# The attention's steps go between halves of the input projection's units, and the scan of layer 0 takes two modulation units a head

## What is computed

```python
sh1, sc1, g1, sh2, sc2, g2 = split(silu(c) @ w_mod + b_mod)     # the modulation, per layer
h = modulate(rms_norm(x), sh1, sc1);  hc = the same of the context
ua, us, um = split_in(h @ w_in)       # attention, short convolution, scan
# attention (4 heads): q from rms_norm(ua[:256]) @ w_uq, k and v from rms_norm(ua[256:384]) @ w_ukv,
#   32 further columns, rotated, are the same for all heads' keys
y_att = softmax(q k^T * scale) v       # over 512 keys (context and x)
# short convolution: gate_b, gate_c, val = split(us)
y_sc = gate_b * dwconv(gate_c * val)
# scan (8 heads of 64, 2 groups, chunks of 128): z, xbc, dt = split(um)
xs, B, C = split(silu(dwconv(xbc) + bias));  la = -softplus(dt + bias) * exp(a_log)
cs = cumsum(la) in a chunk
y = (C B^T * exp(cs_i - cs_j)) (xs * dt) + C state * exp(cs), in both directions
y_ssd = norm((y + d * xs) * silu(z))
x = x + g1 * rms_norm(concat(y_att, y_sc, y_ssd) @ w_out)
x = x + g2 * rms_norm(square(relu(h2 @ w_ff1)) @ w_ff2)
```

## Time and profile before

| what | value |
|---|---|
| time, median of 3 runs | 1649.65 us (1649.46 to 1651.49) |
| the profiled execution | 1653.87 us, its span 1652.1 us |
| mean granted clock of TensorE | 0.962 |
| busy: PE, DVE, ACT, POOL | 93%, 60%, 55%, 4% of the span |
| layer 0: input projection's units from bc on | 69.4 to 161.6 us |
| layer 0: attention, and the scan to its last pair | to 216.3, and to 274 us |
| layer 1: attention | 820.3 to 855.5 us |

### The profile page before, as it was taken

How to read it: one execution, slowest core, us unless ns; L and a number is a source line. 1 busy time by engine, 2 the same in 40 slices (tenths; PEclk the granted TensorE clock), 3 DMA queues, 4 the chain that set the end, 5 groups by cost and what they waited for, 6 DMA issues and landing times.

```text
span 1652.1 us, 25531 instructions
## 1 busy us (share of the span) xinstructions
PE 1530.2 (93%) x10131; PEld 1281.4 (78%) x10131; DVE 985.0 (60%) x1579; ACT 911.5 (55%) x1506; POOL 71.6 (4%) x106
## 2 busy tenths in 40 slices
PE   5999988979999999979988899998999999888887
PEld 3687445748888888838855799998999999888787
DVE  2463568484343434474767766667776767577555
ACT  5653656463241323454565655556786868377745
POOL 3000023000000000000002000000000000001200
PEclk9999889989999999999987999999999999999899
DMA  7731435332523232342316566553644434343332
GB/s 248 231 102 51 153 128 180 127 128 77 178 80 99 101 103 99 110 131 83 123 31 200 179 210 198 194 190 128 217 147 154 154 128 154 103 153 105 100 102 77
DMA packets 223639, 225.38 MB, mean 136 GB/s; under 512 B 8234, under 2 KB 222064, under 8 KB 223472
## 3 DMA queue, kind: packets, MB, share of 16 engines
q1 hardware_dynamic: 222816, 223.63, 41.9%
q0 software_dynamic: 704, 0.12, 0.0%
HBM read 222.68 MB, written 1.05 MB: 135 GB/s over the span
## 4 chain that ended last, share of the span: by engine, by line
PE 75%; DVE 12%; ACT 10%; issue 2%; DMA 1%; SPq 0%; POOL 0%; DVEq 0%; ACTq 0%; POOLq 0%
PE bank L1046 21%; PE bank L1048 21%; PE bank L1047 21%; PE bank L1094 2%; ACT SH L1724 2%; ACT whi L1588 1%; DVE wlo L2151 1%; PE bank L1252 1%; PE bank L1412 1%; DVE AP L2715 1%; PE bank L1440 1%; PE bank L1367 1%; ACT AP L2005 1%; DMA raw<-in_w_out_dram 1%; PE bank L1345 1%
## 5 line engine op out<-in xcount | busy, mean ns | idle before, releaser
L2151 DVE TENSOR_TENSOR wlo<-raw,whi 128x1024 fp32r<-128x1024 f32 (+2 forms) x322 | 388.2, 1209 | 260.0 <-ACT whi L1588 255.2
L1588 ACT ACTIVATE whi<-raw 128x1024 fp32r<-128x1024 f32 (+2 forms) x322 | 336.0, 1046 | 273.2 <-PE bank L1048 251.4
L1046 PE MATMUL bank<-HH,whi 128*128 128x512 f32 (+2 forms) x640 | 245.8, 384 | 18.3 <-DVE HL L2173 15.2
L1047 PE MATMUL bank<-HL,whi 128*128 128x512 f32 (+2 forms) x640 | 241.7, 378 | 0.0
L1048 PE MATMUL bank<-HH,wlo 128*128 128x512 f32 (+2 forms) x640 | 241.4, 377 | 0.0
L1046 PE MATMUL bank<-HA,whi 128*128 128x256 f32 x576 | 166.1, 288 | 13.5 <-DVE LA L2173 5.2
L1047 PE MATMUL bank<-LA,whi 128*128 128x256 f32 x576 | 163.0, 283 | 0.0
L1048 PE MATMUL bank<-HA,wlo 128*128 128x256 f32 x576 | 162.9, 283 | 0.0
L1046 PEld LDWEIGHTS bank<-HH,whi 128*128 128x128 f32 (+1 forms) x640 | 120.8, 189 | 47.9 <-issue 16.6
L1048 PEld LDWEIGHTS bank<-HH,wlo 128*128 128x128 f32 (+1 forms) x640 | 120.9, 189 | 23.5 <-issue 0.5
L1047 PEld LDWEIGHTS bank<-HL,whi 128*128 128x128 f32 (+1 forms) x640 | 121.2, 189 | 22.6 <-issue 0.9
(11 more groups left out here) (375 smaller groups left out, 3141.8 us busy)
## 6 DMA issues: line engine op xcount, KB each, us to landing
raw<-in_w_ff_dram SPq DMA_DIRECT2D x64, 1024.0 KB, 5.4
raw<-in_w_mod_dram SPq DMA_DIRECT2D x48, 1024.0 KB, 5.3
raw<-in_a_w_in_dram SPq DMA_DIRECT2D x40, 1024.0 KB, 5.1
raw<-in_w_in_dram SPq DMA_DIRECT2D x18, 1024.0 KB, 5.4
raw<-in_b_w_in_dram SPq DMA_DIRECT2D x9, 1024.0 KB, 5.3
raw<-in_w_out_dram SPq DMA_DIRECT2D x8, 1024.0 KB, 5.3
raw<-in_ple_w_gate_dram SPq DMA_DIRECT2D x8, 1024.0 KB, 5.2
raw<-in_a_w_out_dram SPq DMA_DIRECT2D x4, 1024.0 KB, 5.1
```

The source lines that it names most:

```text
L1046: nc.tensor.matmul(o, wh, xh, start=start, stop=False, skip_group_check=shared)
L1047: nc.tensor.matmul(o, wh, xl, start=False, stop=False, skip_group_check=shared)
L1588: f(whi[h % HALF_SLOTS][:, 0:n], raw[u.id % RAW_SLOTS][:, (h % 2) * n:(h % 2) * n + n], ACT.Copy)\
L2151: v.tensor_tensor(wlo[h % HALF_SLOTS][:, 0:n], raw[u.id % RAW_SLOTS][:, (h % 2) * n:(h % 2) * n + n], whi[h % HALF_SLOTS][:, 0:n].bitcast( ...
```

## The change

- `mla_square` stands behind bc and `mla_norm` behind xs0, each a unit earlier.
- `mla_proj` is split into `mla_q` and `mla_k`, between the halves of xs1, and `mla_v`, between the halves of gc, with `ssd_cs` part 0. Two heads' keys share a bank, in two halves of 64 partitions.
- `ssd_dt` stands behind xs1, `ssd_cs` part 1 behind gc.
- The steps of `mla_att` stand between and behind the halves of val, gb, z0 and, in layer 0, z1; then `ssd_tok`.
- The seven fillers of layer 0's attention are gone; after the states and after each head 1 to 7 of its scan stand two. 17 stand in this scan instead of 9, and one fewer in its second feed-forward product.
- In layer 1, C is projected, convolved and multiplied for x alone.
- gate_b is no more copied by ACT: DVE multiplies by the bank, behind the convolution, and z0's silu waits for this.
- QT, KT, VV, PR and PT, TP and GC have other places in memory; POOL fills TP's pads in a memset of its own.

Its core as a diff:

```diff
 FILL = {
-    "mla": ((1, (1, 8)), (0, (1, 24))),
+    "win": ((0, (1, 8)), (0, (1, 24))),
+    "odd": ((0, (1, 8)), (0, (1, 24))),
     "g": ((1, (1, 8)), (1, (1, 20))),
-    "head": ((1, (1, 8)), (1, (1, 20))),
+    "head": ((2, (1, 8)), (1, (1, 20))),
...
-        fm(w, 0, COL_XBC + 512, 256, two, "win", (l, "bc"), x, [ALL] * 2)
-        fm(w, 0, COL_XBC, 256, two, "win", (l, "xs0"), x, [ALL] * 2)
+        win(COL_XBC + 512, "bc", [ALL, t1])
         steps.append(("mla_square", l))
-        fm(w, 0, COL_XBC + 256, 256, two, "win", (l, "xs1"), x, [ALL] * 2)
+        win(COL_XBC, "xs0", [ALL] * 2)
         steps.append(("mla_norm", l))
-        fm(w, 0, COL_GC, 256, two, "win", (l, "gc"), x, [t1] * 2)
-        fm(w, 0, COL_VAL, 256, two, "win", (l, "val"), x, [t1] * 2)
+        win(COL_XBC + 256, "xs1", [ALL] * 2, ("mla_q", l), ("mla_k", l))
         if l == 0:
             steps.append(("consts",))
         steps.append(("ssd_dt", l))
-        fm(w, 0, COL_GB, 256, two, "win", (l, "gb"), x, [t1] * 2)
-        fm(w, 0, COL_Z, 256, two, "win", (l, "z0"), x, [t1] * 2)
-        steps.append(("ssd_cs", l))
+        win(COL_GC, "gc", [t1] * 2, ("mla_v", l), ("ssd_cs", l, 0))
+        steps.append(("ssd_cs", l, 1))
+        steps.append(step(0))
+        win(COL_VAL, "val", [t1] * 2, step(1))
+        filler(*FILL["win"][l])
+        steps.append(step(2))
         steps.append(("short_conv", l))
-        fm(w, 0, COL_Z + 256, 256, two, "win", (l, "z1"), x, [t1] * 2)
+        win(COL_GB, "gb", [t1] * 2, step(3))
...
+        if l == 0:
+            win(COL_Z + 256, "z1", [t1] * 2, step(7), step(8))
...
-            for h in range(MLA_HEADS):
-                b = acquire(3 + h, (s_kt, (l, h)))
-                nc.tensor.matmul(b[0:NOPE, 0:T], w_ukv[:, h * P:h * P + NOPE], CK, start=True, stop=True)\
-                    .then_inc(*s_mla_k.tick((l, h)))
+            for p in range(MLA_HEADS // 2):
+                b = acquire(3 + p, (s_kt, (l, 2 * p + 1)))
+                for e in (0, 1):
+                    h = 2 * p + e
+                    ins = nc.tensor.matmul(b[NOPE * e:NOPE * e + NOPE, 0:T], w_ukv[:, h * P:h * P + NOPE], CK, start=True, stop=True)
+                ins.then_inc(*s_mla_k.tick((l, 2 * p), (l, 2 * p + 1)))
...
+        def mla_v(l):
+
+            run_late()
+            for j in range(4):
+                act.wait_ge(s_mla_v, s_mla_v.at((l, j)))
+                f(VV[:, j, :], banks[(7, 3, 4, 5)[j]][:, 0:256], ACT.Copy).then_inc(*s_vv.tick((l, j)))
...
+                elif part == "gb":
+                    for bi in (0, 1):
+                        y = YM[:, 2 + bi, :]
+                        v.tensor_tensor(y, y, bank(u, bi), ALU.mult).then_inc(*s_sc.tick((l, bi)))
```

More of the change, by code:

```diff
@@ L528, in lone_mod, with filler @@
         return u
+    fill = [(0, i) for i in range(8, 24)] + [(1, i) for i in range(0, 24)]
+    def filler(n, upto):
+        for _ in range(n):
+            if fill and fill[0] < upto:
+                ll, i = fill.pop(0)
+                mod_units(ll, i, i + 1)
     def w_in_units(l, opening):
@@ L534, in w_in_units, with at_half, win, step @@
             steps.append(("unit", u))
[L535 to L536 removed]
+        att = [(l, 2 * p + e, sg) for p in range(MLA_HEADS // 2) for sg in ((0, 1) if l == 0 else (1,)) for e in (0, 1)]
+        def at_half(part, *here):
+            if part != "z1":
+                steps.append(("split_to", 2 * next_sid() + 1))
+            for step in here:
+                steps.append(step)
+        def win(col, part, t, *here):
+            fm(w, 0, col, 256, two, "win", (l, part), x, t, (lambda: at_half(part, *here)) if here else None)
+        def step(i):
+            return ("mla_att", att, i)
+        win(COL_XBC + 512, "bc", [ALL, t1])
         steps.append(("mla_square", l))
[L538 removed]
+        win(COL_XBC, "xs0", [ALL] * 2)
         steps.append(("mla_norm", l))
[L540 to L541 removed]
+        win(COL_XBC + 256, "xs1", [ALL] * 2, ("mla_q", l), ("mla_k", l))
         if l == 0:
@@ L683, in build @@
             filler(*FILL["head"][l])
+            if h % 2 == 1:
+                filler(*FILL["odd"][l])
         def out_unit(i):
@@ L1534, in _ @@
                 mla_norm(*args)
-            elif kind == "mla_proj":
-                mla_proj(*args)
+            elif kind == "mla_q":
+                mla_q(*args)
+            elif kind == "mla_k":
+                mla_k(*args)
+            elif kind == "mla_v":
+                mla_v(*args)
             elif kind == "mla_att":
@@ L1904, in ssd_dt, with ssd_cs @@
             f(AA[:, 0, :], a_log[:, l, :], ACT.Exp).then_inc(*s_aa.tick(l))
-        def ssd_cs(l):
+        def ssd_cs(l, part):
+            if part == 0:
+                return
             act.wait_ge(s_df, s_df.at(l))
@@ L2245, in unit @@
                             .then_inc(*s_val.tick((l, "val", bi)))
+                elif part == "gb" and u.packed:
+                    y = YM[:, 2:4, SEQ:T]
+                    v.tensor_tensor(y, y, both(bank(u, 1)), ALU.mult).then_inc(*s_sc.tick((l, 0), (l, 1)))
+                elif part == "gb":
+                    for bi in (0, 1):
+                        y = YM[:, 2 + bi, :]
+                        v.tensor_tensor(y, y, bank(u, bi), ALU.mult).then_inc(*s_sc.tick((l, bi)))
                 elif part in ("bc", "xs0", "xs1"):
@@ L2899, in _ @@
                     nc.gpsimd.memset(XP0, 0.0)
-                    nc.gpsimd.memset(XP1, 0.0)
-                    nc.gpsimd.memset(TP, 0.0).then_inc(*s_pads.tick(l))
+                    nc.gpsimd.memset(XP1, 0.0).then_inc(*s_pads.tick(l))
+            elif kind == "unit" and args[0].kind == "win" and args[0].key[1] == "xs0":
+                l = args[0].key[0]
+                pool.wait_ge(s_parts, s_parts.at((l, "mix", KC - 1)))
+                nc.gpsimd.memset(TPW, 0.0).then_inc(*s_tp_pads.tick(l))
             elif kind == "att2_second" and args[0][0] == 1:
```

144 lines of the change are left out of this document (78 added, 66 removed).

## The result

The changed kernel takes 1670.83 us in the median of 4 runs (1668.46 to 1677.42), against 1649.84 (1649.46 to 1651.49) for the kernel before. The ratio is 1.0126, with a 95% interval of 1.0099 to 1.0153: slower by 21 us. The forecast was 1668, with a chance of 0.76 for slower. The profiled execution of the changed kernel is its fastest run, 1668.46 us, so the two traces differ by only 14.6 us of span. The four runs of the kernel before lie unusually close together: in the 11 to 23 runs that stand beside the experiments its median is 1650.6 to 1654.7 us, and against those the change costs 16 to 20 us and not 21.

What follows compares the result with a forecast made beforehand. PE's queue was taken to bound the kernel: layer 0 attention 0, its scan +13, ff2 -1.3, layer 1 +6.5, together +18.2, so 1672.1 us on the profiled execution and, 4.2 lower, 1667.9 as median. Range for 8 in 10: 1652 to 1680.

Steps and rivals of the forecast that it cites:

- The wait before `mla_q`: Attention, both layers: PE waits for DVE's queries (QC), 3.6 us in layer 0 and about 2.8 in layer 1.
- The wait before `ssd_cs`: Middle of gc, both layers: PE waits for LA and ACT's VV copies, 8 us in layer 0, about 9 in layer 1.
- the rival on the other side: Faster: PE's work covers the wait before `ssd_cs` in both layers, 25 us less, time 1643; chance of faster 0.17.
- The decision point: The change turns to a gain when the `ssd_cs` stops of both layers together cost less than 7 us.
- The clock behind these waits: Attention, both layers: a slow stretch behind each of the four new waits, 4 us each, 16 in all.
- `mla_k` and the halves of layer 1: Smaller PE work: `mla_k` saves 1.7 us in each layer; in layer 1 bc saves 2.7 and the g matmuls 0.9.
- The scan of layer 0: Eight more modulation units on PE, two in a slot: +13 us, bounds +2 and +18.
- the reason that I gave for the even heads: Layer 0's scan: the pick waits for ACT's mod_row copy, 3.84 us behind the rows; even heads 6.5 instead of 3.17.
- bound by something slower: Rival, layer 0's scan: 4 MB of transfers or DVE's modT banks make a pair of heads 14.5 us: +5, 1673; chance 0.12.
- my own case: The forecast's own case, 1661 to 1674 us, chance 0.52; in layer 0's scan, heads of 6.5 us each.
- The scan of layer 1: Half-width g matmuls give back 0.9 us; modulation order as before, DVE's halved copies under PE.
- The drain at each change of set: ACT's table loads: a skill's rule adds about 1.38 us per change, time near 1676; the sum left it out.

Runs made afterwards that it cites:

- e7: The changed kernel with xs1 whole and ssd_dt (bank 7 instead of 5), mla_q and mla_k behind it: 1654.42 us, ratio 0.9998 to the kernel before.
- e4: The changed kernel with mla_v and both parts of ssd_cs between the halves of val instead of gc, attention's step 0 ahead of them: 1664.08 us.
- e6: The changed kernel with ssd_cs part 0 moved from between the halves of gc to behind gc, mla_v left in place: 1662.90 us.
- e8: e7 with ssd_cs part 0 behind gc and attention's step 0 between its two parts: 1639.88 us, ratio 0.9936 to the kernel before.
- e1: The kernel before, its order kept, with only the change's smaller arithmetic (shared key banks, layer 1's C for x alone): 1648.66 us, ratio 0.9973.
- e2: The changed kernel, but ACT copies a head's modulation rows ahead of the next head's exponentials instead of behind them: 1669.51 us.
- e10: e9 with four of layer 0's modulation units moved from its scan's even heads to behind val, gb, z0 and z1: 1632.72 us, ratio 0.9879.
- e12: e10 with DVE's recurrence back ahead of head 1's modulation units: 1635.79 us, ratio 0.9900 to the kernel before.
- e3: The changed kernel with one modulation unit a head in layer 0's scan, and eight between the units of layer 0's input projection: 1670.82 us.
- e9: e8 with DVE's recurrence (ssd_rec) behind head 1's modulation units instead of ahead of them: 1644.09 us, ratio 0.9925 to the kernel before.
- e11: e1 with DVE's recurrence behind the unit of head 1, as in e9: 1652.25 us, ratio 0.9983.
- e5: The changed kernel with two modulation units ahead of xs1 in each layer, and fewer in the scans (13 instead of 17 in layer 0): 1667.42 us.

## Why the prediction was right, and where it was off

- *The wait before `mla_q`*: 3.6 and 2.8 forecast, 3.17 and 2.69 measured. e7 takes it away.
- *The wait before `ssd_cs`*: 8 and 9 forecast, 6.50 and 5.98 measured, ended by ACT's VV as forecast, and 0.69 and 3.13 for XR just ahead of it. Together these are 7.2 and 9.1, so the sum was met; that the last matmul of the values waits for XR stands in the order shown above the forecast, and the forecast did not price it apart. e7 shows the cause: with the dt chain and the convolution of xs1 beside q's matmuls instead of behind its copies, `ssd_cs` comes 10 us earlier. More cover alone helps less: of the 16.3 us some 14 are left in e4, in other places, and 11 in e6. So the rival on the other side named the right place: two stops and the clock behind them. The decision point held as well: with them smaller (2.0 and 4.4 us), e7 is level with the kernel before, and e8 is faster.
- *The clock behind these waits*: mis-sized. I took 4 us for each of four. Measured were 1.4 and 2.9 in layer 0, and 1.4 and 3.6 in layer 1: 9.3 for 16. A slow stretch often covers part of the wait itself, where nothing is lost: the first of layer 0 begins at 102.1 us, 0.6 before its wait ends, and the second of layer 1 lasts from 812.1 to 825.8, with the wait of 5.98 inside. These 6.7 us are most of the 3.5 and 3.8 us by which the two attention stretches came out better than forecast.
- *`mla_k` and the halves of layer 1*: 7.4 us of work by e1, 7.0 forecast (1.7 + 1.7 + 2.7 + 0.9).
- *The scan of layer 0*: +13.7 for +13. From the scan's first row to head 3 it is 7.1 us longer (30.1 for 23.0), where 3.9 were forecast, and from head 3 to head 7 6.5 longer (25.7 for 19.2), where 9.2 were (2 x 3.3 + 2 x 1.3). Some 3 us of this are one slow stretch behind the wait for the recurrence, which both kernels have and which now falls ahead of head 3 and not behind it; without it the two parts are +4.0 and +9.3. The last slot is 0.1 longer for a forecast of -0.1, but by luck: the wait of 4.04 is gone altogether, where I took 1.4 off, and 3.4 us of clock, for which the sum has no term, come in its place. Nor is the reason that I gave for the even heads the only one. The picks behind ACT's copies do wait, as e2's edit shows, only a transfer stands right behind them: the rival "bound by something slower" and my own case were both true at once, at 6.3 and 6.5 us a head. The units do not cost alike: by e10 and e12 the four in the even heads cost 9.6 and 9.8 us, and a scan with 13 units (56.8, 58.8) is only some 2 to 5 slower than one with 9 (54.0, 55.1 in e3).
- *The scan of layer 1*: -0.9 forecast, +3.9 measured. This was not foreseen. The clock is at its lower level for 21 us at a stretch, where before there were two with full clock between:

```profile
884.00:894.00 10.00, 9.37 (x58) 5.05 (x58) 5.39 (x15) 2.19 (x7) 2.18 (x3) 0.50 0.48 156
894.00:905.00 11.00, 11.00 (x63) 5.94 (x63) 2.41 (x7) 5.10 (x14) 2.90 (x4) 0.53 0.60 192
```

  The same stretch of before:

```profile
873.00:880.00 7.00, 7.00 (x47) 3.82 (x39) 4.55 (x12) 2.02 (x6) 2.17 (x3) 0.52 0.48 154
880.00:890.00 10.00, 8.08 (x73) 4.80 (x69) 3.10 (x8) 5.40 (x15) 2.92 (x4) 1.00 0.88 280
890.00:901.00 11.00, 9.74 (x58) 6.17 (x59) 10.25 (x20) 9.58 (x23) 5.01 (x5) 0.53 0.68 220
```

  The instructions of this stretch are the same but for the narrower products of C and B, and the wait ahead of it is 2.3 us (2.9 before). Over the scan PE loses 10.9 us to the clock (7.5 before) and is idle for 8.4 (6.7 before). The loss of time shows only at the end: the last pair but one starts 39.8 us behind the first row (39.7 before), and the last one 8.0 us later, where it was 4.1. A chain leads there. PE ends a modulation unit at 904.41 us, at the lower clock; SP issues a transfer of w_out's weights at 904.46, which lands at 910.29; and ACT waits for it before the exponentials of the last head:

```profile
902.47 1.94 PE L1126 MATMUL bank<-raw,silu_c_wide 128*32 128x256 f32 x16
...
910.37 1.06 ACT L1632 ACTIVATE whi<-raw 128x1024 fp32r<-128x1024 f32 x1 [1.82 <-DMA raw<-in_w_out_dram]
911.46 0.38 ACT L1999 ACTIVATE EC<-bank 128x256 f32<-128x256 f32 x1
```

  The same scan comes in two lengths in the other kernels. It takes 42.9 us from its first row to its last pair in e1, 43.9 in e4, 43.0 in e6, 43.7 in e7 and 43.5 in e10, and 47.0 in e2, e3 and e9, 47.1 in e8, 48.2 in e11 and 45.8 in e12. Each of the long ones has 17 to 21 us of low clock at a stretch, as here, and of the short ones none has more than 11 at a stretch. Only e5, with two units fewer there, takes 43.6 us with 27 us of low clock. e1 and e11 both have the order of before and differ in the place of the recurrence alone. So it goes with the clock and is not peculiar to the change; what decides between the two was not tried, and with one trace a kernel it can be chance.
- *From profile to median*: I carried the distance of the kernel before (4.2 us) over. The changed kernel's profiled execution was 2.4 below its median and not above it, so +14.6 by the traces became +21 in the medians. The time of 1668 was thus met with two errors against each other: the sum of the trace was 3.6 too high, and the step to the median 6.6 too low. So the place and rough size of the new waits were right by the mechanism; that the time came within 3 us was luck.

The drain at each change of set, which the Trainium skill gives in "ScalarE: Activation LUTs", What ACT_TABLE_LOAD costs, was rightly left out. In layer 0 of the changed kernel ACT's copies end at 116.97 us and the table load starts at 116.99, the Exp starts 1.30 us behind the start of its load (127.06, 128.36) and the silus 1.29 behind theirs (129.83, 131.12): there is no room for a further 1.38 in any of them.

## What to carry to other kernels

Work that is moved between the units of a matmul-bound stage brings its producers' queues along: write down for each moved step when the last of its inputs leaves ACT and DVE in their order, and place the step by that, not by the free place on PE. Two fillers in one place are not twice one: the second waits for copies, reduces and transfers that a lone one found done here. Put one in each place, and move the chain's start (here dt and the convolution ahead of q, 16 us) before adding cover at its end (8 us alone).

## What the runs showed of the hardware

- Matmuls that write the two halves of a bank's partitions run together: eight records of 512 columns took 1.94 us instead of 3.6.
- The loss to TensorE's clock differs between kernels far more than the waits explain: 37.3 us in e10 and 52.4 in e12, which differ in the place of one step, with 118.9 and 116.3 us of PE's idle in the whole span. The mean granted clock also moves between executions of one kernel, from 0.959 to 0.969 in e8.
- The scan of layer 1 alone took 43 to 44 or 46 to 48 us with nearly the same instructions.
- Runs of one kernel spread over up to 20 us (e4: 1655.32 to 1675.22). A gain of a few microseconds in this kernel is hardly shown by medians of 4 to 10 runs; it has to be found in the stretches of the traces, and better in two kernels than in one.
